# Sharing out the low parts of the gate rows between the scalar engine and GpSimd

## What is computed

```python
best_s, best_c = lax.top_k(cand_s, PEER_TOPK)            # 8 heads x 16 experts for each token
expert_idx = jnp.take_along_axis(cand_i, best_c, axis=-1)
gate = jax.nn.softmax(best_s, axis=-1)
u_sel, v_sel = expert_u[expert_idx], expert_v[expert_idx]
act = jax.nn.gelu(jnp.einsum('nhkd,nd->nhk', u_sel, x_blk), approximate=False)
return jnp.einsum('nhk,nhkd->nd', (gate * act), v_sel)
```

## Time and profile before

| | |
|---|---|
| three timed runs | 1755.76, 1756.73, 1756.87 us (median 1756.73) |
| the profiled execution | 1754.75 us |
| its span from first to last instruction | 1753.0 us |
| granted TensorE clock, mean | 0.996 |
| busy share PE, DVE, ACT, POOL | 98%, 74%, 44%, 44% |
| the 128 steps | from 508 to about 1213 us of the span |
| hot steps | from 583.5 us (first L1456) to 1161.5 us (last L1362) |

### The profile page before, as it was taken

How to read it: one execution, slowest core, us unless ns; L and a number is a source line. 1 busy time by engine, 2 the same in 40 slices (tenths; PEclk the granted TensorE clock), 3 DMA queues, 4 the chain that set the end, 5 groups by cost and what they waited for, 6 DMA issues and landing times.

```text
span 1753.0 us, 24582 instructions
## 1 busy us (share of the span) xinstructions
PE 1709.8 (98%) x9066; PEld 1519.8 (87%) x9066; DVE 1292.4 (74%) x1844; ACT 771.7 (44%) x1092; POOL 767.4 (44%) x486
## 2 busy tenths in 40 slices
PE   7999999998999999999999999999999999999997
PEld 5778778887889999999999999999888888888885
DVE  2555511115999899989999789886787787787786
ACT  5444433234333566746667466654223323323322
POOL 3332334332311455665666578881533333332330
PEclk9999999999999999999999999999999999999998
DMA  5222223322235777777777988888999999999992
GB/s 156 73 60 84 60 73 95 108 73 72 84 118 191 221 247 247 240 251 283 259 248 254 327 306 299 292 305 318 376 370 377 360 346 378 361 357 360 368 343 103
DMA packets 212293, 413.80 MB, mean 236 GB/s; under 512 B 11504, under 2 KB 150800, under 8 KB 206864
## 3 DMA queue, kind: packets, MB, share of 16 engines
q1 hardware_dynamic: 156880, 253.78, 41.8%
q0 software_dynamic: 36864, 134.23, 21.4%
q10 hardware_dynamic: 18496, 25.19, 4.1%
HBM read 360.73 MB, written 52.43 MB: 236 GB/s over the span
## 4 chain that ended last, share of the span: by engine, by line
PE 80%; DVE 10%; POOL 3%; DMA 2%; ACT 2%; issue 2%; ACTq 0%; SPq 0%; DVEq 0%; POOLq 0%
PE psum L1205 28%; PE psum L229 22%; PE psum L1146 21%; PE psum L1136 4%; DVE ring L1468 2%; DVE ul L1393 2%; PE psum L1173 2%; DMA ring<-in_expert_u,index 1%; PE psum L303 1%; PE psum L289 1%; POOL ring L1352 1%; POOL grid L1371 1%; PE psum L423 1%; PE psum L317 1%; DVE hot L1456 1%
## 5 line engine op out<-in xcount | busy, mean ns | idle before, releaser
L1146 PE MATMUL psum<-xTh,uh 128*128 128x384 f32 x1024 | 354.1, 346 | 9.8 <-DVE ul L1393 9.3
L1146 PE MATMUL psum<-xTl,uh 128*128 128x384 f32 x1024 | 343.3, 335 | 0.0
L1146 PE MATMUL psum<-xTh,ul 128*128 128x384 f32 x1024 | 343.3, 335 | 0.0
L1352 POOL DMA_INDIRECT ring<-in_expert_v,index x128 | 176.9, 1382 | 311.0 <-DVE acc L1473 269.0
L212 POOL TENSOR_TENSOR wl<-raw,wh 128x1024 fp32r<-128x1024 f32 x72 | 172.5, 2403 | 320.9 <-ACT wh L485 320.9
L1205 PE MATMUL psum<-vh,dwh 128*128 128x512 f32 x768 | 298.8, 389 | 1.2 <-DVE dwl L1486 1.2
L1205 PE MATMUL psum<-vl,dwh 128*128 128x512 f32 x768 | 298.8, 389 | 0.0
L1205 PE MATMUL psum<-vh,dwl 128*128 128x512 f32 x768 | 298.8, 389 | 0.0
L1278 ACT ACTIVATE vh<-v_raw 128x4096 fp32r<-128x4096 f32 x31 | 112.6, 3634 | 340.2 <-PE psum L1205 339.8
L1352 POOL DMA_INDIRECT ring<-in_expert_u,index x128 | 172.9, 1351 | 152.6 <-DVE ring L1468 80.1
L1468 DVE SCALAR_TENSOR_TENSOR ring<-ring,x 128x1024 f32<-128x1024 f32 x120 | 199.8, 1678 | 12.3 <-DMA ring<-in_expert_u,index 11.0
(11 more groups left out here) (206 smaller groups left out, 2893.3 us busy)
## 6 DMA issues: line engine op xcount, KB each, us to landing
u_raw<-in_expert_u SPq DMA_DIRECT2D x128, 512.0 KB, 4.5
v_raw<-in_expert_v SPq DMA_DIRECT2D x30, 2048.0 KB, 12.2
expert_act<-hb ACTq DMA_DIRECT2D x128, 192.0 KB, 3.9
expert_gate<-grid SPq DMA_DIRECT2D x12, 2048.0 KB, 7.2
dh<-expert_act SPq DMA_DIRECT2D x32, 768.0 KB, 4.4
dg<-expert_gate SPq DMA_DIRECT2D x32, 768.0 KB, 6.7
raw<-in_w_in SPq DMA_DIRECT2D x40, 512.0 KB, 3.8
raw<-in_w_q SPq DMA_DIRECT2D x16, 512.0 KB, 4.0
```

What stands on the lines that cost most here:

```text
L1146: last = nc.tensor.matmul(zb[s][:, 0:DT], w[s][:, c, :], x[:, c, 0:DT], start=(c == 0 and i == 0), stop=(c == C - 1 and i == 2))
L1352: nc.gpsimd.indirect_dma_start(out=ring[k][:], out_offset=None, in_=tables[x // SLOTS], in_offset=bass.IndirectOffsetOnAxis(ap=index[:, x ...
```

## The change

Of the eight tokens of a batch, ACT now makes the high parts of tokens 4 to 7 first and then signals POOL (`hot_hi`), makes those of tokens 0 to 3, each with an increment of a new semaphore `hot_low4`, waits on that semaphore for its own four results (the low part overwrites the row that the high part was read from), and makes the low parts of tokens 0 to 3 itself, one instruction for each. POOL makes the low parts of tokens 4 to 7 alone. PE waits for `hot_low4` in place of `hot_hi`.

```diff
@@ spread
             if half == 0:
                 pe.wait_ge(hot_ready[s], q + (x // 4 + 1))
-                pe.wait_ge(hot_hi[s], q + (x // 4 + 1))
+                pe.wait_ge(hot_low4[s], q * 5 + (x // 4 * 5 + 5))
                 pe.wait_ge(hot_lo[s], q + (x // 4 + 1))
@@ hi
             act.wait_ge(S["hot_eq"], k + 1)
-            for n in range(8):
+            def high_part(n):
                 t = 8 * k + n
-                last = nc.scalar.activation(hot[s][:, n, 1, :], hot[s][:, n, 2, :].bitcast(F), ACT.Copy,
+                return nc.scalar.activation(hot[s][:, n, 1, :], hot[s][:, n, 2, :].bitcast(F), ACT.Copy,
                                             scale=gate_hi[:, t:t + 1].bitcast(F))
+
+            for n in range(4, 8):
+                last = high_part(n)
             last.then_inc(hot_hi[s], 1)
+            for n in range(4):
+                high_part(n).then_inc(hot_low4[s], 1)
+
+            act.wait_ge(hot_low4[s], k // 2 * 5 + 4)
+            for n in range(4):
+                t = 8 * k + n
+                last = nc.scalar.activation(hot[s][:, n, 2, :], hot[s][:, n, 2, :].bitcast(F), ACT.Copy,
+                                            scale=gate_lo[:, t:t + 1])
+            last.then_inc(hot_low4[s], 1)
@@ lo
             pool.wait_ge(hot_hi[s], k // 2 + 1)
-            low_ = hot[s][:, :, 2, :]
-            nc.gpsimd.tensor_tensor(low_, low_.bitcast(F), gate_lo[:, 8 * k:8 * k + 8].unsqueeze(2).broadcast_to([P, 8, KEYS]),
+            low_ = hot[s][:, 4:8, 2, :]
+            nc.gpsimd.tensor_tensor(low_, low_.bitcast(F), gate_lo[:, 8 * k + 4:8 * k + 8].unsqueeze(2).broadcast_to([P, 4, KEYS]),
                                     ALU.mult).then_inc(hot_lo[s], 1)
```

More of the change, by code:

```diff
@@ L1034, in experts_program @@
     sums = [psum[:, i * T:(i + 1) * T] for i in range(2 * DB)]
-    ut_hi, ut_lo, u_mm, h_done, h_out, hot_ready, hot_hi, hot_lo, g_full = (
+    ut_hi, ut_lo, u_mm, h_done, h_out, hot_ready, hot_hi, hot_low4, hot_lo, g_full = (
         [sem(f"{n}{i}") for i in range(2)] for n in (
-            "ut_hi", "ut_lo", "u_mm", "h_done", "h_out", "hot_ready", "hot_hi", "hot_lo", "g_full"))
+            "ut_hi", "ut_lo", "u_mm", "h_done", "h_out", "hot_ready", "hot_hi", "hot_low4", "hot_lo", "g_full"))
     S = {n: sem(n) for n in (
```

## The result

The changed kernel takes 1761.38 us against 1756.30 us for the kernel before (medians of 20 runs each); the ratio is 1.0027, 95% interval 1.0019 to 1.0035, or 3.3 to 6.1 us slower. The forecast was slower, by 11.3 us. Its direction held and its size did not.

What follows compares the result with a forecast made beforehand. PE, busy 98% of the span, was taken to bound the kernel, with `ul` deciding its stalls. Terms 7.2 + 3.6 + 1.8 + 1.2 + 0.5 - 3.0 = +11.3 us gave 1768.0 us on the median; range 1755 to 1777.

Steps and rivals of the forecast that it cites:

- term B: Steps 26, 34, 62, 70: L1362 follows the gather back to back, ahead of DVE's waiting row; 4 x 0.9 = +3.6 us.
- term A: Eight hot steps of blocks 0 and 1: L1362 comes due during held L1458, goes ahead of DVE's row; +7.2 us.
- DVE's `ul` is what a gain or loss has to go through: PE's loads ahead of `products` wait 8.7 us, all for DVE's `ul`; whether it comes earlier or later decides.
- POOL's half takes 1.0 us and is due 1.35 us after ACT's first: POOL's low part for 512 elements takes 1.0 us, due 1.35 us after ACT's first high part, not 2.51.
- Term C: ACT's added work makes GELU and all behind it 0.9 us later; not hidden in steps 40 and 76, +1.8 us.
- In an ordinary hot step this is hidden: Outside steps 40 and 76, ACT's 0.9 us delay costs nothing; the gather moves by 0.2 us at most.
- Terms on the edge: Steps 44, 54, 80, gather's end and signal within 0.12 us: +1.2 us; step 50, L1362 ahead of a row: +0.5 us.
- The third block: POOL in arrears, L1362 holds rows 1.0 us instead of 1.9; stalls of steps 100, 116, 118 go, -3.0 us.
- Rival 1: A waiting POOL operation yields to DVE's next one, no loss in A, B, D's three steps; 1756.0 us, no change; chance 0.15.
- Rival 2: POOL also wins the lock in 16 narrow steps like 20, 12.2 us more, giving 1780.2 us; chance 0.12.
- Rival 3: POOL's relief is worth more, rows always in the ring, lock costs nothing: -4.9 us, 1753.6 or 1751.8 us; chance 0.08.

Runs made afterwards that it cites:

- e11: e9 but with the change's early signal, POOL signalled after four high parts; 1749.40 against 1755.76 us for the kernel before.
- e1: The changed kernel, but ACT signals POOL only after all eight high parts; 1753.66 against 1755.65 us for the kernel before.
- e4: Kernel before plus ACT's wait and four added instructions copying high parts onto themselves, POOL's low parts whole; 1758.91 against 1755.65 us.
- e2: The changed kernel without ACT's low parts (tokens 0 to 3 left out), early signal kept; 1756.47 against 1755.65 us for the kernel before.
- e3: Kernel before with POOL's low parts for tokens 4 to 7 alone, late signal, the others left out; 1751.98 against 1755.65 us.
- e9: Changed kernel with late signal, ACT's low parts a step later, POOL's gather behind DVE's row in the first two blocks' hot steps; 1748.40 against 1757.75 us (kernel before).
- e10: Kernel before with only the gather's wait for DVE's row in hot steps of the first two blocks; 1755.38 against 1757.75 us.

## Why the prediction was right in direction and wrong in size

The direction and the main mechanism held. The size was 11.3 us against 5.1 in the times and 6.3 by steps, mostly because term B (+3.6 us) measured 0.1 and term A (+7.2 us) measured 4.9.

- *DVE's `ul` is what a gain or loss has to go through.* Right. Before and after, in every step from 14 to 120 that is longer than its unbroken work the products start 0.05 or 0.06 us behind the end of `ul`.
- *POOL's half takes 1.0 us and is due 1.35 us after ACT's first.* Right: 1.03 us, and 630.97 - 629.63 = 1.34 in step 22.
- *Term A, due while L1458 runs, +7.2 us.* Right in mechanism, too large. It happened in six of the eight steps named, at 0.86, 0.86 and 0.83 us (steps 22, 38 and 42) and 0.86, 0.83 and 0.70 (58, 74 and 78): 4.9 us. In steps 38 and 74 it took ACT's lateness as well, as told below. In steps 30 and 66 the second one-hot is no longer held by the gather, since POOL's relief moves the gathers: the late-signal version without ACT's low parts loses the same 0.2 us stall there. I had kept the before's collisions fixed.
- *Term B, back to back behind the gather, +3.6 us.* This is the step that failed. In its four steps the time moved by -0.26, +0.11, +0.21 and +0.08 us, 0.1 in all. I took steps 26, 34, 62 and 70 to be like step 98. In 34, 62 and 70 the low part did come back to back with the row waiting, and the row went first. They differ from step 98 in one thing that the rows showed: the gather of step 98 takes 1.31 us, it ran at once; the gather of step 26 takes 1.44, it had first been held by DVE. (Step 26 itself went another way in the changed kernel: its gather came 2.8 us later in the step than before, behind the row.) In all ten profiles before e11 together I count 72 places in which POOL issues its low part back to back with a gather while a DVE row, issued behind the gather's start, has waited for 0.9 us or more. Where the gather had run at once (1.29 to 1.32 us) POOL kept the lock, 53 of 53. Where it had itself been held (1.44 to 2.34 us) DVE's row got it, 19 of 19. The three such places of e11 are of the first kind and POOL kept the lock. The kernel before has a place of the second kind too, which I had overlooked: in step 112 the row was issued 0.05 us ahead of L1362 behind a gather of 1.45 us, and L1362 took 2.92 us. The changed kernel's own example of the first kind, in the third block, POOL and then DVE:

```profile
1066.20 1.32 POOL L1383 TENSOR_TENSOR grid<-parts 128x512 f32<-128x512 f32 x1
1067.44 1.06 POOL L1374 TENSOR_TENSOR hot<-hot,gate_lo 128x512 fp32r<-128x512 f32 x1
```

```profile
1066.31 3.28 DVE L1480 SCALAR_TENSOR_TENSOR ring<-ring,x 128x1024 f32<-128x1024 f32 x1
```

- The Trainium skill ("SBUF — State Buffer", Who interferes with whom) gives the lock to whichever issues first. That held in the 19 and not in the 53, where the row had been issued 0.9 to 1.2 us ahead. So its price for term B, 0, which the prediction gives and sets aside, is near what was measured, and the five places of the third block on which I set it aside were all of one kind.
- *Term C, ACT, +1.8 us.* Right where it was placed: the steps 40 to 42 and 76 to 78 together are 0.94 and 0.90 us longer. The 2.5 us that the prediction works out beside it takes each ACT instruction at its full length; in a run they start 0.29 us apart. But there the 0.97 and 0.94 fall in steps 41 and 77, as a term A that the forecast counted as lying inside C. In e1 and e4, which have no term A there, the same steps are 0.8 and 0.9 us longer by ACT alone. The chain of waits of the changed kernel through step 40, which answers to the earlier trace rows:

```profile
736.16 0.38 ACT hb L1237
...
740.91 0.93 ACT uh L1230
741.84 0.02 issue
741.87 1.23 DVE ul L1405
```

- "In an ordinary hot step this is hidden" was too simple. ACT's low parts move the gather of the even spread by up to 0.9 us (in step 20 it starts 8.02 us behind the first one-hot, without them, in e2, 7.13), and with it which DVE operation it meets. ACT's low parts cost 1.4 us by steps with the late signal and 4.4 us with the early one. The difference arises mostly in steps 39 and 75, where together they bring a term A that either alone does not (in step 39 +0.87 with both, -0.30 with the early signal alone, 0.0 with ACT's low parts alone). In step 39 DVE's key picking also meets the later gather; DVE's timeline:

```profile
726.24 2.20 DVE L1422 TENSOR_TENSOR eq<-eq,picks 128x1024 f32<-128x1024 f32 x1
```

- *Terms on the edge, +1.7 us.* Too small: steps 44 to 46 and 80 to 82 gave 1.44 and 1.43 us, as terms A after all (0.6 of each is in e3 too, without the early signal); the step behind 54 gave nothing, and the boundary gave -0.3.
- *The third block, -3.0 us.* Right, step for step: 0.49, 1.85 and 0.65 us in steps 100, 116 and 118.
- *Rival 1*, that a waiting POOL operation yields, was true for B and false for A. *Rival 2* did not happen: rows of 20, 24 and 28 never had more than 2.33 us. *Rival 3* missed what happens when the lock costs nothing: there is a gain, 6 us by steps in e9 and e11. Half of it is the third block's 3.0, which rival 3 had and the forecast too; the other half is DVE's hot steps with fewer meetings. The 1.5 us at the boundary did not go.

By terms: A 4.9 for 7.2, B 0.1 for 3.6, C 1.8 for 1.8, the edge and the boundary 2.6 for 1.7, the third block -3.0 for -3.0, and steps 30, 31, 38, 66, 67 and 74 -0.2; 6.3 us for 11.3.

## What to carry to other kernels

Where POOL and DVE exclude each other, ask of every signal to POOL which DVE operation is running when it comes, and which is next: a POOL operation that becomes ready early can cost more than one that is late and off the path. Give POOL its work behind DVE's last critical operation, if it is short enough to be done before DVE's next (it paid with low parts of 1.0 us in e9, and not clearly with 1.9 us in e10), and put added ACT work into the step where ACT waits, not ahead of what others wait for. When a trace is used to say who wins a lock, compare the cases down to whether each had itself been held, not by the order of issue alone. And when collisions are counted from a trace of before, expect them to move: of twelve places in terms A and B six lost what was forecast.

## What the runs showed of the hardware

A gather or low part of POOL that comes due while a DVE operation with two inputs in SBUF runs, with another such operation next on DVE, goes ahead of that next one: so in 405 of 406 places of the eleven profiles. The exception is the gather of step 24 of the changed kernel, due 0.18 us behind the start of the second one-hot, which took 3.34 us and let the row by.

Of back-to-back POOL operations the second let a waiting DVE operation pass only where the first had itself been held (19 of 19). A POOL operation that ran at once hands the lock to POOL's next one, issued 0.04 to 0.08 us ahead of its own end, over a DVE operation that has waited for 0.9 to 1.2 us (53 of 53). Whether it is the holding that decides, or that DVE's next operation follows at once on the one that held the gather, can't be told apart here: in all 19 cases both are so. Taking the gather out of DVE's hot steps left L1458 and the row of steps 20 and 22 at 1.22 us each (e9), so the rest of the row's 2.33 us, and of the 2.33 us of L1458 in steps like 22, was this lock.
